# Two residual blocks on one core: the second norm's factor applied at eviction, step-size and convolved-channel projections in other matmul forms, gate and pool weights loaded later

## What is computed

```python
def first_block(...):
    mod = silu(c) @ w_ada + b_ada            # 2048 -> 6 x 2048: sh1, sc1, gt1, sh2, sc2, gt2
    h = rmsnorm(x, g_norm_mix) * (1 + sc1) + sh1
    xr, gr, xp = split(h @ w_in)             # 3 x 1024
    ...  # causal conv, RG-LRU with gates xh @ w_rg_a, xh @ w_rg_i; pooled xp @ w_pool
    x = x + gt1 * (y @ w_out)
    h = rmsnorm(x, g_norm_ffn) * (1 + sc2) + sh2
    x = x + gt2 * ((silu(h @ w_ffn_gate) * (h @ w_ffn_up)) @ w_ffn_down)
    return rmsnorm(x, g_norm_final)

def second_block(h, p, ...):
    proj = rmsnorm(h, attn_norm_g) @ w_in_2  # 2048 -> z 2048, xbc 3072, dt 32, q 2048, k 512, v 512
    xbc = silu(causal_dwconv(xbc, conv_w, conv_b))   # 4 taps along the tokens, per channel
    dt = softplus(dt_raw + dt_bias)
    ...  # y_ssm from xbc, dt, z; y_att: attention over a window of 128 tokens
    h = h + concat(y_ssm, y_att) @ w_out_2
    ...  # convolved FFN, then a gate from another rmsnorm of h
```

## Time and profile before

| | us |
|---|---|
| median of 3 runs | 2695.87 |
| lowest and highest run | 2694.89, 2697.79 |
| the profiled execution's own time | 2694.49 |
| its span from first to last instruction | 2692.8 |
| TensorE busy | 2603.6 (97%) |
| VectorE busy | 1660.3 (62%) |
| ScalarE busy | 1245.9 (46%) |
| granted TensorE clock, mean | 0.981 of 2.4 GHz |

### The profile page before, as it was taken

One profiled execution on the slowest core, in us unless ns is written; L12 is line 12 of the kernel. 1 busy time (PEld: TensorE's weight loads), 2 busy tenths in 40 slices (PEclk: granted clock), 3 DMA queues, 4 the chain that ended last, 5 costly groups with the idle time before them and its releaser, 6 DMA issues.

```text
span 2692.8 us, 33691 instructions
## 1 busy us (share of the span) xinstructions
PE 2603.6 (97%) x13006; PEld 2181.9 (81%) x13006; DVE 1660.3 (62%) x1958; ACT 1245.9 (46%) x1591; POOL 5.6 (0%) x24
## 2 busy tenths in 40 slices
PE   7699889999999999989999999999999999999998
PEld 3599777888888888878899988888888888888877
DVE  4798897664544444463876667555666666644444
ACT  2246335444444434443566556445555555544453
POOL 0000000000000000000000000000000000000000
PEclk8899999999999999988999999999999999999999
DMA  9997897875555555544533543555555555555554
GB/s 355 349 368 256 322 362 240 274 264 180 190 190 191 172 190 187 184 150 142 175 123 110 160 137 125 187 188 188 186 183 183 183 185 187 188 184 186 191 194 141
DMA packets 350000, 548.47 MB, mean 204 GB/s; under 512 B 18480, under 2 KB 200768, under 8 KB 349248
## 3 DMA queue, kind: packets, MB, share of 16 engines
q1 hardware_dynamic: 349888, 546.90, 60.0%
HBM read 544.74 MB, written 2.10 MB: 203 GB/s over the span
## 4 chain that ended last, share of the span: by engine, by line
PE 83%; DVE 7%; DMA 4%; ACT 3%; issue 2%; SPq 1%; ACTq 0%; DVEq 0%
PE pair L1151 23%; PE pair L1153 23%; PE pair L1152 23%; DMA mod_raw<-in_w_ada 3%; PE pair L1126 2%; PE pair L1127 2%; PE pair L1128 2%; DVE mod_acc L1968 2%; DMA mod_more<-in_w_ada 1%; DVE w_lo L1737 1%; PE pair L1664 1%; ACT w_hi L626 1%; DVE mod_acc L1994 1%; PE misc L1599 1%; PE misc L1717 1%
## 5 line engine op out<-in xcount | busy, mean ns | idle before, releaser
L1737 DVE TENSOR_TENSOR w_lo<-raw,w_hi 128x1024 fp32r<-128x1024 f32 x848 | 1017.4, 1204 | 879.2 <-ACT w_hi L626 878.0
L626 ACT ACTIVATE w_hi<-raw 128x1024 fp32r<-128x1024 f32 x848 | 882.1, 1043 | 1134.3 <-PE pair L1153 1022.9
L1151 PE MATMUL pair<-w_hi,a_hi 128*128 128x512 f32 x1856 | 733.9, 395 | 8.7 <-DVE w_lo L1737 3.5
L1153 PE MATMUL pair<-w_hi,a_lo 128*128 128x512 f32 x1856 | 725.6, 391 | 0.0
L1152 PE MATMUL pair<-w_lo,a_hi 128*128 128x512 f32 x1856 | 724.9, 391 | 0.0
L1151 PEld LDWEIGHTS pair<-w_hi,a_hi 128*128 128x128 f32 x1856 | 350.4, 189 | 82.2 <-issue 6.7
L1153 PEld LDWEIGHTS pair<-w_hi,a_lo 128*128 128x128 f32 x1856 | 350.0, 189 | 74.1
L1152 PEld LDWEIGHTS pair<-w_lo,a_hi 128*128 128x128 f32 x1856 | 350.6, 189 | 71.7 <-issue 1.0
L1151 PE MATMUL pair<-w_hi,hid_hi 128*128 128x512 f32 x704 | 274.7, 390 | 0.0
L1153 PE MATMUL pair<-w_hi,hid_lo 128*128 128x512 f32 x704 | 274.0, 389 | 0.0
L1152 PE MATMUL pair<-w_lo,hid_hi 128*128 128x512 f32 x704 | 273.9, 389 | 0.0
(11 more groups left out here) (367 smaller groups left out, 2191.1 us busy)
## 6 DMA issues: line engine op xcount, KB each, us to landing
raw<-in_w_in SPq DMA_DIRECT2D x88, 1024.0 KB, 5.4
raw<-in_w_up SPq DMA_DIRECT2D x176, 512.0 KB, 4.4
mod_raw<-in_w_ada SPq DMA_DIRECT2D x160, 512.0 KB, 6.5
raw<-in_w_out SPq DMA_DIRECT2D x48, 1024.0 KB, 5.0
raw<-in_w_ffn_gate SPq DMA_DIRECT2D x88, 512.0 KB, 3.6
raw<-in_w_ffn_up SPq DMA_DIRECT2D x88, 512.0 KB, 4.6
raw<-in_w_ffn_down SPq DMA_DIRECT2D x32, 1024.0 KB, 5.1
raw<-in_w_down SPq DMA_DIRECT2D x32, 1024.0 KB, 5.0
```

What stands on the lines that cost most here:

```text
L626: run(w_hi[:, h % HALF_SLOTS, 0:n, :], raw[:, h // 2 % RAW_SLOTS, at0:at0 + n, :], ACT.Copy).then_inc(hi_ready, 1)
L1151: pe.matmul(o, hi[:, own], w_hi[:, slot, kk, :], start=(h == kk == 0), stop=False)
L1153: mm = pe.matmul(o, lo[:, own], w_hi[:, slot, kk, :], start=False, stop=(h == ph.halves - 1 and kk == n - 1))
L1737: dve.tensor_tensor(w_lo[:, slot, 0:n, :], raw[:, h // 2 % RAW_SLOTS, at0:at0 + n, :], w_hi[:, slot, 0:n, :].bitcast(F32), ALU.subtract).t ...
```

## The change

- **Norm 2.** x is multiplied by g_final (`fin_row`, broadcast by a DMA behind the loads of FFN block 10) on VectorE chunk by chunk; the transposed chunk is split at once with the gain of the attention norm as a per-partition factor (`turned_high`, `turned_low`). Sums of squares of x and of x·g_final are taken on ScalarE (Square with an accumulator). Three chunks are done inside down1, the last beside w_in2's block 0. The per-token factor `scale` is applied when ScalarE evicts each block of w_in2 (`evict`: two of 128x512 instead of one of 128x1024). x times `rstd` follows at place 7 of block 0. `weigh_squares`, `spread` and the transposes of g_final are gone.
- **gt2's row** comes in four parts of four transposes at the start of down1's blocks.
- **dt.** `w_dt_two` (64 columns, hi beside lo) is held and 256 tokens move: 32 matmuls behind block 1; ScalarE evicts, two small matmuls in block 2 turn the result, and VectorE adds the parts.
- **xbc.** The six blocks are in tokens form; ScalarE evicts into `xbc_t`, and eight transposes (`turn_xbc`) behind half 0 of the next block put it channel-major into the other half of `pair`; `conv_bias` and the taps follow one place later than before.
- **Gate and pool loads** go out before the loads of block 2 of w_in instead of block 1; GpSimd clears `gates_w` after `vec_turned`, no longer after the modulation product.

```diff
-    pool.wait_ge(mod_mm, MOD_FIRST)
+    pool.wait_ge(vec_turned, 1)
     pool.memset(gates_w[:], 0.0).then_inc(zeroed, 1)
...
-    sp.wait_ge(zeroed, 2)
...
-    sp.dma_start(pool_w[:], d["w_pool"][0].rearrange("g (k p) n -> p (g k) n", p=P)).then_inc(mixw_landed, 16)
     for b in range(1, w_in.blocks):
+        if b == 2:
+            sp.wait_ge(zeroed, 2)
+            for n, w in enumerate((d["w_rg_a"][0], d["w_rg_i"][0])):
+                for e in range(2):
+                    sp.dma_start(gates_w[64 * e:64 * e + 64, n, :, 64 * e:64 * e + 64],
+                                 w.rearrange("(m e) i j -> e i m j", e=2)[e]).then_inc(mixw_landed, 16)
+            sp.dma_start(pool_w[:], d["w_pool"][0].rearrange("g (k p) n -> p (g k) n", p=P)).then_inc(mixw_landed, 16)
         load_beside(w_in, b, plain(d["w_in"][0], bass.ds(w_in_cols[b], COLS)))
     for b in range(w_out.blocks):
...
+    sp.wait_ge(x_new, w_out.blocks)
+    sp.dma_start(fin_row[:], d["g_norm_final"][None, :].to_broadcast([P, D])).then_inc(broadcast_landed, 16)
...
+    def sums_of(b, parts, n0):
+        for t in range(T):
+            act.wait_ge(n_ssq, SSQ_DONE[1] + n0 + t)
+            run(misc[:, 3, :], x[:, t, b * COLS:(b + 1) * COLS], ACT.Square,
+                accum_out=parts[:, t * XB + b:t * XB + b + 1]).then_inc(n_ssq, 1)
+    def norm2_beside(b, place):
+        if place == SUMS2_AT:
+            act.wait_ge(x_new, X_BEFORE[2] + b + 1)
+            sums_of(b, ssq_parts, 2 * T * b)
+        elif place == SUMS2_FIN_AT:
+            act.wait_ge(fin_x, b + 1)
+            sums_of(b, ssq_fin, 2 * T * b + T)
+        elif place == HALVES2_AT:
+            turned_high(2, b, g_att)
...
-    norm_end(2, g_both)
+    def beside_down1(b, place):
+        if b:
+            norm2_beside(b - 1, place)
+        elif place == LAST_HIDDEN + 1:
+            hidden_high(up1.blocks, 1)
+        if place == (GT2_AT if b else LAST_HIDDEN + 1):
+            act.wait_ge(gt2_row, b + 1)
+            if b:
+                act.wait_ge(res_ready, w_out.blocks + b)
+            run(gt2[:], misc[:, 2, :], ACT.Copy).then_inc(row_ready, 1)
+    stream(down1, None, w_in2, beside=beside_down1)
...
+            if b == 0:
+                norm2_beside(XB - 1, n)
+                if n in (ROOT2_AT, ROOT2_AT + 1):
+                    root(ROOTS[2][n - ROOT2_AT])
+            if b == 2 and n == 0:
+                act.wait_ge(dt_acc, 1)
+                run(dt_f[0:2 * SH, :], misc[0:2 * SH, 2, 0:S], ACT.Copy).then_inc(dt_ev, 1)
...
+    def evict(dst, c, func=ACT.Copy):
+        for t in range(T):
+            ins = run(dst[:, t], pair[:, c, t, :], func, scale=scale[:, t:t + 1])
+        return ins
...
-        run(q_t[:, :, 8 * b:8 * b + 8, :].rearrange("p t h e -> p t (h e)"), pair[:, b % 2], ACT.Copy).then_inc(qkv_ev, 1)
+        if b == 0:
+            act.wait_ge(n_rstd, 2)
+        evict(q_t[:, :, 8 * b:8 * b + 8, :].rearrange("p t h e -> p t (h e)"), b % 2).then_inc(qkv_ev, 1)
...
+    def convolution(place):
+        j = place // w_in2.halves
+        if j and place % w_in2.halves == CONV2_AT:
+            act.wait_ge(xbc_turned, j)
+            conv_bias((B_XBC + j - 1) % 2, 4 * j - 4, cw2[:, (CONV - 1) * XBC:], cb2, xbc, c2_bias)
...
     for b in range(B_XBC, B_Z):
         j = b - B_XBC
-        mixer2(b, attention)
-        conv_bias(b % 2, 4 * j, cw2[:, (CONV - 1) * XBC:], cb2, xbc, c2_bias)
+        mixer2(b, attention_beside)
+        if j:
+            act.wait_ge(xbc_turned, j)
+        evict(xbc_t, b % 2).then_inc(qkv_ev, 1)
         if j:
             act.wait_ge(c2_tap, 12 * j)
             run(flat(xbc[:, 4 * j - 4:4 * j, :]), flat(xbc[:, 4 * j - 4:4 * j, :]), ACT.Silu).then_inc(xbc_ev, 1)
...
-    def weigh_squares(b):
...
+            if n == 2 and h == 0:
+                gt2_rows(b)
             if h == 2 and b:
...
-                    weigh_squares(b - 2)
...
+    def gt2_rows(b):
+        pe.wait_ge(mod_ready, 10)
+        if b:
+            pe.wait_ge(row_ready, b + 1)
+        for m in range(4):
+            mm = pe.transpose(misc[:, 2, m * P:(m + 1) * P], mod[:, 5 * KC + 4 * b + m:5 * KC + 4 * b + m + 1].to_broadcast([P, P]), ident[:])
+        mm.then_inc(gt2_row, 1)
...
-    rows_of(mod[:, 5 * KC:6 * KC], row_mm)
...
-    norm_end(2)
...
+    def last_norm2(h):
+        if h == TURN2_AT:
+            turn_block(2, XB - 1)
+    def steps_out(h):
+        if h == 1:
+            pe.wait_ge(dt_ev, 1)
+            for t in range(T):
+                mm = pe.matmul(misc[:, 3, t * 2 * SH:(t + 1) * 2 * SH], dt_f[0:2 * SH, t * P:(t + 1) * P], ident[0:2 * SH, 0:2 * SH],
+                               start=True, stop=True, skip_group_check=True)
+            mm.then_inc(dt_mm, 1)
...
-            rows_of(g_fin, fin_mm)
+        tokens(w_in2, b, b % 2, normed, beside_v if b == B_V else last_norm2 if b == 0 else steps_out if b == 2 else None,
+               normed_yet(2) if b == 0 else None)
         if b == 1:
...
+            pe.wait_ge(dt_lo, 2)
+            for k in range(KC):
+                two = w_dt_two[:, k:k + 2, :].rearrange("p k h -> p (k h)")
+                pe.matmul(misc[:, 2, 0:S], two, a_hi[:, k, :], start=(k == 0), stop=False)
+                mm = pe.matmul(misc[:, 2, 0:S], two, a_lo[:, k, :], start=False, stop=(k == KC - 1))
+            mm.then_inc(dt_acc, 1)
+    pe.wait_ge(dt_x, 1)
+    def turn_xbc(j):
+        pe.wait_ge(qkv_ev, B_XBC + j)
+        for m in range(4):
...
-                    pe.matmul(o, a_hi[:, k, own], w_dt_hi[:, k, :], start=(k == 0), stop=False, skip_group_check=True)
-                    pe.matmul(o, a_hi[:, k, own], w_dt_lo[:, k, :], start=False, stop=False, skip_group_check=True)
-                    mm = pe.matmul(o, a_lo[:, k, own], w_dt_hi[:, k, :], start=False, stop=(k == KC - 1), skip_group_check=True)
-            mm.then_inc(dt_mm, 1)
-    pe.wait_ge(dt_x, 1)
+                mm = pe.transpose(pair[:, (B_XBC + j - 1) % 2, m // 2, m % 2 * S + t * P:m % 2 * S + (t + 1) * P],
+                                  xbc_t[:, t, m * P:(m + 1) * P], ident[:])
+        mm.then_inc(xbc_turned, 1)
...
         else:
             pe.wait_ge(c2_tap, 12 * (j - 1))
-        features(w_in2, b, b % 2, a_hi, a_lo, lambda h: attention(j * w_in2.halves + h))
+        def beside(h):
+            if j and h == TURN_XBC_AT:
+                turn_xbc(j)
+            attention(j * w_in2.halves + h)
+        tokens(w_in2, b, b % 2, normed, beside)
...
+    def add_final(b, c):
+        cols = bass.ds(b * COLS, COLS)
+        dve.wait_ge(row_ready, b + 2)
+        dve.tensor_tensor(pair[:, c], pair[:, c], gt2[:, None, :].to_broadcast([P, T, COLS]), ALU.mult).then_inc(res_ready, 1)
+        dve.wait_ge(res_ready, w_out.blocks + b + 1)
+        dve.tensor_tensor(x[:, :, cols], x[:, :, cols], pair[:, c], ALU.add).then_inc(x_new, 1)
...
+    def norm2_beside(b, place):
+        if place == FIN2_AT:
+            if b == 0:
+                dve.wait_ge(broadcast_landed, 16)
+            dve.wait_ge(n_ssq, SSQ_DONE[1] + 2 * T * b + T)
+            cols = slice(b * COLS, (b + 1) * COLS)
+            dve.tensor_tensor(x[:, :, cols], x[:, :, cols], fin_row[:, None, cols].to_broadcast([P, T, COLS]), ALU.mult).then_inc(fin_x, 1)
+        elif place == HALVES2_AT:
+            turned_low(2, b, g_att)
...
+    def norm2_factor(place):
+        if place == ROOT2_AT:
+            dve.wait_ge(n_ssq, SSQ_DONE[2])
+            done(dve.tensor_reduce(ssq, ssq_parts.rearrange("p (t b) -> p t b", t=T), AX.X, ALU.add))
+            done(dve.tensor_reduce(squared, ssq_fin.rearrange("p (t b) -> p t b", t=T), AX.X, ALU.add))
+            done.wait()
+            inverse_root(ssq, rstd, n_var, n_std, ROOTS[2][0])
+            done(dve.tensor_tensor(squared, squared, rstd, ALU.mult))
+            done.wait()
+            done(dve.tensor_tensor(squared, squared, rstd, ALU.mult))
+            done.wait()
+            inverse_root(squared, scale, n_var, n_std, ROOTS[2][1])
+            dve.tensor_tensor(scale, scale, rstd, ALU.mult).then_inc(n_rstd, 1)
+        elif place == ROOT2_AT + 2:
+            for t in range(T):
+                dve.tensor_scalar(x[:, t, :], x[:, t, :], rstd[:, t:t + 1], None, ALU.mult)
...
     def convolution(place):
         j = place // w_in2.halves - 1
-        if j >= 0:
-            conv_taps(place % w_in2.halves, (B_XBC + j) % 2, 4 * j, cw2, CONV, XBC, xbc, c2_bias, c2_tap, 12 * j)
+        if j >= 0 and place % w_in2.halves >= CONV2_AT:
+            conv_taps(place % w_in2.halves - CONV2_AT, (B_XBC + j) % 2, 4 * j, cw2, CONV, XBC, xbc, c2_bias, c2_tap, 12 * j)
```

More of the change, by code:

```diff
@@ L886, in _ @@
             stream(up1, finish_up1, down1, peel=1, evict=hidden_high)
-            act.wait_ge(row_mm, 2)
-            run(row[:], flat(misc[:]), ACT.Copy).then_inc(row_ready, 1)
-            act.wait_ge(n_gain, 1)
-            stream(down1, norm_beside(2, g_both), w_in2,
```

(7 more changed lines are left out.)

186 lines of the change are left out of this document (78 added, 108 removed).

## The result

| | us |
|---|---|
| changed kernel, median of 4 runs | 2652.4 (2647.56 to 2653.23) |
| kernel before, median beside it | 2695.38 |
| ratio | 0.9839, 95% interval 0.9821 to 0.9857 |
| profiled execution after: own time, span | 2653.23, 2651.5 |
| forecast | 2648.0, range 2639 to 2666 |

The kernel is 43 us faster (1.6%), inside the range and 4.4 us above the point. The two profiled executions differ by 41.3 us (2694.5 against 2653.2).

The account below looks back on a forecast made before the run. TensorE, busy 97% of the span, was taken to set the pace nearly everywhere, except at w_in's start. Terms -16.8 - 3.4 - 14.6 - 7.9 - 5.2 = -47.9 us gave 2646.6, 2648.0 as a median, range 2639 to 2666.

Parts of the forecast that it names:

- Norm 2 and the weighings, -20.2: Joint of down1 and w_in2, -16.8 us with block 0 starting early; two weighings gone from inside down1, -3.4.
- the stall: Before the last chunk's eight transposes in w_in2's block 0: TensorE waits 0.5 us for VectorE's product with the gain.
- The rival that norm 2's tail shows in block 0: w_in2 block 0: 9 us of VectorE's new work show as waits, 2657 us in all; chance 0.07.
- Step sizes, -14.6: w_in2 blocks 1 and 2: 32 products replace 96 small ones, -12.6 us; clock behind them recovers, 2.0.
- Convolved channels, -7.9: Six xbc blocks: form -7.5 us, transposes +5.2, three block-edge gaps -3.7, clock 1.9 taken once.
- the net of form and transposes: Six xbc blocks: tokens form gains 7.5 us, added transposes cost 5.2, so 2.3 us faster.
- -9.5 with the clock back twice: Fast bound of the convolved channels' term: the missing clock of the gap stretches is regained twice instead of once.
- the bound of the step sizes: w_in2 blocks 1 and 2: slow bound -12.5 us, if the clock dip comes all the same.
- Loads, -5.2: Start of w_in: gate and pool loads moved behind block 1 remove VectorE's 5.2 us wait for a modulation load.
- the load hole is worth nothing: Rival at w_in's start: transfers are already full and moved bytes are paid back at once, 2653 us; chance 0.12.
- no gap of SyncE up to 115: Sign at w_in's start: SyncE no longer stands waiting until 115 us once the gate loads are moved.
- The round trip: Rival in six xbc blocks: TensorE waits some 1.2 us each at the transposes for evictions, 2661 us; chance 0.14.

Follow-up runs that it names:

- form_only: The kernel before with the xbc blocks alone in tokens form (evictions without a factor, eight transposes, bias steps and taps one place later): 2685.99 us, ratio 0.9968.
- bias_later: The kernel before, features form and no transposes, with only ScalarE's four bias steps moved to place 1 of the next block, taps one place later: 2686.15 us, ratio 0.9968.
- loads_only: The kernel before with only the gate and pool loads and the clearing of gates_w moved as in the change: 2693.17 us, ratio 0.9990.

## Why the prediction was right, and where it wasn't

**Norm 2 and the weighings, -20.2: right.** Measured -20.6 and -20.7. The first joint is gapless, the stall was 0.25 and not 0.5, and block 0 with its edge took 23.1 where 23.3 was forecast. The 16 gt2 transposes moved from ahead of down1 (-1.6) into it (0.4 to 0.5 a block), as said. The rival that norm 2's tail shows in block 0 didn't come; block 0 has one wait, the 0.25.

**Step sizes, -14.6: right.** -14.6 in the changed kernel, -14.1 alone. The two small products that turn the result back cost about 1.0 us and not 0.5: block 2 takes 22.7 us where block 3, without them, takes 21.8.

**Convolved channels, -7.9: right in sum, by luck, mis-sized inside.** With the form alone it is -7.9, in the changed kernel -6.7. Two misses of about 1.5 us cancel. One is the net of form and transposes, forecast as -2.3, of which 0.8 is left (form_only against bias_later). By the rows a block should have been 1.25 shorter in the new form, and the one without transposes was 1.04 shorter; over six blocks that is 1.3 of the miss, while a group of transposes cost 0.85 where 0.88 was counted. The other is the clock. The forecast took one stretch at 0.95, 1.9 us; the next one shows 0.95 too, 1.8 us more, and both are at 1.00 in bias_later:

```profile
1463.10:1499.10 36.00, 34.77 (x284) 33.94 (x282) 21.63 (x49) 22.04 (x46) 0.00 (x0) 0.95 0.37 116
```

Then the factor's evictions, which I had priced at 0.686 but not set against the shorter ones that they replace, go with 1.3 less gain. The Trainium skill's formula (TensorE: Matmul & The Clock Gate, Back-to-back issue gap), which the page gives for the gap of an isolated matmul, would have made the block 0.25 shorter; 1.04 was measured, nearer to the rows. That ScalarE's bias steps made the gaps was argued, and bias_later shows it. The place was wrong, since the product that waited stands 13 us behind the edge. That the transposes give TensorE work ahead of it was right for the changed kernel. The bound "-9.5 with the clock back twice" should have been -9.8, and the bound of the step sizes -12.6; neither matters for the range.

**Loads, -5.2: too much, and here a step failed.** Over the start, w_in and w_out the changed kernel gained 0.3 and 0.7 us in two executions, and loads_only gained 2.4 by the medians. By the traces this term is what the forecast missed: 4.5 to 4.9 us of gain that didn't come, where the result is 4.4 above the point. The first half of it held: the raw load went out at once, and VectorE's wait of 5.2 us is gone. The step that failed is the payback, "3.9 us of transfer, where I take transfers to have slack". The place had none (a share of 0.99 in the kernel before), the bytes took 6.5 us and not 3.9, and VectorE's wait came back in block 1 with 5.9 us. That is the mechanism of the rival "the load hole is worth nothing", moved bytes paid back at once, and its price too: 2653 there, 2652.4 measured. Of the signs named, "no gap of SyncE up to 115" failed as well, because the next entry of the queue waits for VectorE; the order of SyncE shows that wait. This gap holds nobody up, but it is room: with the loads in it the kernel gains 5.8 us.

**The other rivals.** The round trip (evict, transpose) did not hold TensorE: the evictions ended 0.6 us ahead, near the 0.5 of the forecast. The clock stayed at 1.00 in the xbc stage. What stays open: norm 2's part was not run alone, because its factor needs every block of w_in2 in tokens form, so its size is read from the two traces; and the 1.6 us steps of the FFN and the last phase were not pursued.
